# Weight splitting on GpSimd: whole units against pieces of two blocks

## The reference, cut to what matters

```python
h = rmsnorm(x, norm_mix)
proj = h @ w_in                       # q | k | v | g_ret | x_lru | y_lru | g_a | g_b
o, S_new = retention(rope(q), rope(k), v, S_ret)       # 4 heads, decay-weighted
ret_branch = (silu(g_ret) * groupnorm(o)) @ w_ret_out
xc = causal_conv(x_lru, conv_w, conv_b)
hl = rg_lru(xc, wa, wx, lambda)       # gated linear recurrence, block-diagonal gates
lru_branch = (gelu(y_lru) * hl) @ w_lru_out
x = x + (sigmoid(g_a) * ret_branch + sigmoid(g_b) * lru_branch) @ w_o
gu = rmsnorm(x, norm_ffn) @ w_gate_up
x = x + (silu(gu[:, :D_FF]) * gu[:, D_FF:]) @ w_down
```

## Time and profile before

| what | us |
|---|---|
| median of three runs | 2663.13 |
| lowest and highest | 2660.95, 2665.93 |
| the profiled execution, whole | 2665.94 |
| its span, first to last instruction | 2663.7 |
| PE busy | 2478.1 (93%) |
| DVE busy | 1368.6 (51%) |
| POOL busy | 1401.2 (53%) |
| ACT busy | 597.9 (22%) |

### The profile page before, as it was taken

How to read it: one execution, slowest core, us unless ns; L and a number is a source line. 1 busy time by engine, 2 the same in 40 slices (tenths; PEclk the granted TensorE clock), 3 DMA queues, 4 the chain that set the end, 5 groups by cost and what they waited for, 6 DMA issues and landing times.

```text
span 2663.7 us, 51524 instructions
## 1 busy us (share of the span) xinstructions
PE 2478.1 (93%) x19572; PEld 2406.2 (90%) x19572; DVE 1368.6 (51%) x1693; ACT 597.9 (22%) x849; POOL 1401.2 (53%) x845
## 2 busy tenths in 40 slices
PE   7799999978989999999997999999879999999997
PEld 7699989978889999999996999898779898999997
DVE  6455555587565543123254565655785656330333
ACT  2313131224251111001113132221434311110111
POOL 4254535444556656666652545454445565556664
PEclk9899999988999999999998999999999999999999
DMA  4535455312222222222245445362112222223222
GB/s 161 174 127 198 145 178 169 111 60 69 77 78 90 92 79 87 87 95 90 92 135 202 150 156 182 131 196 80 60 61 84 86 91 87 79 85 97 88 87 86
DMA packets 113009, 298.42 MB, mean 112 GB/s; under 512 B 11681, under 2 KB 12449, under 8 KB 112865
## 3 DMA queue, kind: packets, MB, share of 16 engines
q1 hardware_dynamic: 60480, 199.78, 23.1%
q10 hardware_dynamic: 52384, 96.56, 10.5%
HBM read 255.92 MB, written 40.38 MB: 111 GB/s over the span
## 4 chain that ended last, share of the span: by engine, by line
PE 76%; DVE 12%; DVEq 6%; issue 2%; ACTq 1%; ACT 1%; DMA 0%; POOL 0%; POOLq 0%
PE proj L310 69%; PE aux L463 2%; DVEq L1067 2%; DVE scratch L882 2%; PE aux L471 2%; PE aux L486 1%; PE aux L433 1%; DVE scratch L969 1%; DVE split_scratch L675 1%; DVE scratch L973 1%; DVEq L881 1%; ACTq L1386 1%; DVEq L972 1%; DVE scratch L668 1%; PE aux L450 1%
## 5 line engine op out<-in xcount | busy, mean ns | idle before, releaser
L296 POOL TENSOR_SCALAR w_high<-w_raw 128x1024 fp32r<-128x1024 f32 (+3 forms) x420 | 434.4, 1034 | 1176.9 <-PE proj L310 1167.0
L298 POOL TENSOR_TENSOR w_low<-w_raw,w_high 128x1024 fp32r<-128x1024 f32 (+3 forms) x420 | 966.4, 2301 | 62.2 <-issue 1.1
L310 PE MATMUL proj<-x_high,w_high 128*128 128x260 f32 x4096 | 849.1, 289 | 83.5 <-DVE scratch L951 35.2
L310 PE MATMUL proj<-x_high,w_low 128*128 128x260 f32 x4096 | 837.2, 286 | 0.0
L310 PE MATMUL proj<-x_low,w_high 128*128 128x260 f32 x4096 | 836.1, 286 | 0.0
L310 PEld LDWEIGHTS proj<-x_high,w_high 128*128 128x128 f32 x4096 | 645.2, 193 | 101.7 <-issue 49.1
L310 PE MATMUL proj<-split_scratch,w_high 128*128 128x260 f32 x4000 | 654.7, 286 | 38.2 <-DVE scratch L855 17.6
L310 PEld LDWEIGHTS proj<-x_high,w_low 128*128 128x128 f32 x4096 | 643.4, 192 | 0.0
L310 PEld LDWEIGHTS proj<-x_low,w_high 128*128 128x128 f32 x4096 | 643.4, 192 | 0.0
L310 PEld LDWEIGHTS proj<-split_scratch,w_high 128*128 128x128 f32 x4000 | 556.0, 191 | 43.7 <-DVE scratch L855 18.9
L310 PE MATMUL proj<-split_scratch,w_low 128*128 128x260 f32 x2000 | 406.4, 285 | 0.0
(11 more groups left out here) (145 smaller groups left out, 1941.9 us busy)
## 6 DMA issues: line engine op xcount, KB each, us to landing
w_raw<-in_wstream SPq DMA_DIRECT2D x252, 512.0 KB, 3.3
scratch<-in_sret ACTq DMA_DIRECT2D x64, 512.0 KB, 5.8
out_ret_s<-scratch ACTq DMA_DIRECT2D x64, 512.0 KB, 4.3
w_raw<-in_wstream SPq DMA_DIRECT2D x72, 448.0 KB, 3.2
w_raw<-in_wstream SPq DMA_DIRECT2D x48, 384.0 KB, 3.0
scratch<-v_rows ACTq DMA_DIRECT2D x64, 256.0 KB, 3.7
w_raw<-in_wstream SPq DMA_DIRECT2D x48, 320.0 KB, 2.7
out_ret_p<-scratch ACTq DMA_DIRECT2D x8, 512.0 KB, 2.8
```

Of the source, the lines that this page charges most:

```text
L296: pool.tensor_scalar(WH[:, j, w], WR[:, j, w], 1.0, 0.0, ALU.mult, ALU.add)
L298: pool.tensor_tensor(WL[:, j, w], WR[:, j, w], WH[:, j, w].bitcast(F32), ALU.subtract).then_inc(s["w_split"], 1)
L310: m = pe.matmul(out, wt[:, w, blk * P:(blk + 1) * P], x[xi], start=first and n == 0, stop=last and n == 2)
```

## The change

GpSimd no longer splits a unit in two instructions. A loop goes over the unit in pieces of two blocks (256 columns); each piece has its own rounding (TENSOR_SCALAR), drain and subtraction (TENSOR_TENSOR). A unit of odd size ends with a piece of one block. Only the last subtraction raises `w_split`; the waits ahead of the unit, the buffers and every other engine stay as they are.

```diff
+PIECE = 2
@@ in block.gpsimd
                         for k, n in enumerate(blocks):
-                            j, w = (base + k) % 2, slice(0, n * P)
+                            j = (base + k) % 2
                             u = layer * UNITS + base + k + i * len(blocks)
                             pool.wait_ge(s["w_used"], u + 2)
                             pool.wait_ge(w_ld[j], ...)
                             pool.sem_inc(s["go_pool"], 1)
-                            pool.tensor_scalar(WH[:, j, w], WR[:, j, w], 1.0, 0.0, ALU.mult, ALU.add)
-                            pool.drain()
-                            pool.tensor_tensor(WL[:, j, w], WR[:, j, w], WH[:, j, w].bitcast(F32),
-                                               ALU.subtract).then_inc(s["w_split"], 1)
+                            for b in range(0, n, PIECE):
+                                p = slice(b * P, min(b + PIECE, n) * P)
+                                pool.tensor_scalar(WH[:, j, p], WR[:, j, p], 1.0, 0.0, ALU.mult, ALU.add)
+                                pool.drain()
+                                m = pool.tensor_tensor(WL[:, j, p], WR[:, j, p], WH[:, j, p].bitcast(F32),
+                                                       ALU.subtract)
+                            m.then_inc(s["w_split"], 1)
```

## The result

The changed kernel takes 2836.08 us (median of four, 2835.01 to 2838.45) against 2663.83 us before: ratio 1.065, 95% interval 1.063 to 1.067. So it is 172 us slower; 99 were forecast, with 2675 to 2850 as the range.

A forecast was written before the change was run, and what follows sets the result against it. PE sets the time, and POOL's idle time cannot be saved up because each split has a deadline. Stage losses of 134 us less 35 returned by DVE gave 99, so 2762 us; range 2675 to 2850.

The forecast's parts named there:

- w_down: Feed-forward w_down stage: 32 units of 6 with no spare lose 0.98 us each, 31 us; units of 5 nothing.
- merge: Merge stage: 48 units of 7 lose 0.74 us each after 1.03 spare, 36 us.
- the cost of a further piece: Each further POOL piece adds drain and fixed parts of rounding and subtraction, less overlap: 0.49 us, ends 0.22 and 0.60.
- lru_out: lru_out stage: 14 units of 5 with 0.35 us spare lose 0.63 each, 9 us.
- gate and up: Gate and up stage: 44 pairs lose 0.57 us each, contending DVE instructions included, 25 us.
- heads: Heads stage: about 60 directly following units lose 0.02 us plus 0.4 for DVE each, 25 us.
- the return of 35: Shorter DVE waits give back 1.3 us for each of 16 y-tiles, plus 14 for convolution and w_o: 35 us.
- upper rival: Whole kernel much slower, 2870 us: 0.60 us a piece, 212 us lost, DVE gains nothing; chance 0.10.
- The rest: mostly hidden, 8: Remaining stages, bound by DVE: growth mostly hidden by POOL idle times of over 2.1 us; 8 us put down.
- The turn-round in gate and up: Unavoidable POOL idle time between splits, 0.66 us read from w_down; leaves gate and up 1.45 us spare a unit.
- faster: Whole kernel at 2631 us: further pieces cost near 0.22 us, DVE's shorter waits return 47; chance 0.09.
- The estimate of 0.41 a piece and 78 us: POOL's three reads a piece cost 0.26 us, with the drain 0.41; stage sums about 78 us instead of 134.

The follow-up runs named there:

- the early signal: Changed kernel, but TensorE may begin a unit when its first piece is split and waits for the whole ahead of the third block: 2629.23 us, ratio 0.9869.
- fixed-only kernel: Kernel before, units split whole, with two or three pairs of tiny GpSimd instructions and drains behind each split, before its signal: 2878.18 us, ratio 1.0795.

## Why the prediction was right in kind and low in size

The mechanism held. POOL's idle time could not be saved up: the early signal, which leaves POOL's work as it is and moves only the deadline, takes the loss away on balance (w_down keeps 4.6 and the merge 5.7 us). The durations were right (0.41 and 0.74 expected; 0.41 and 0.74 measured), and so was the cost of a further piece (0.49 against 0.51). PE waits for POOL 227 times for 176.8 us (some 250 times and over 100 us forecast). L1096 takes 0.70 and L1046 0.75 (below 1.3 forecast), L969 0.22 on average (below 1). PE's idle time in 530 to 680 us went from 30.3 to 24.6, so by far less than half.

Term by term, what was forecast and measured: merge 36 and 34.9; lru_out 9 and 9.8; gate and up 25 and 30.7; w_down 31 and 42.9; heads 25 and 51.1; all else 8 less the return of 35, so -27, and 1.0 measured. So the size was low by 73 us, and that it still fell into the range owes something to the range's width: 2836 is nearer to the upper rival's 2875 than to the forecast 2762. But that rival isn't what happened. It asked for 0.60 a piece and no return, and both were otherwise; of its terms for gate and up (54), merge (51), heads (45) and w_down (38), only heads and w_down came near. Two terms hold most of the error, heads (26) and the rest (23), and w_down (12) most of what is left:

- The heads. I gave every contending DVE instruction 0.4 us of POOL's time, from an instruction of 520 columns. The state update has 1024 columns and two SBUF inputs, and holds POOL up by 0.8 to 1.0; halving it gave back 21 of the 26 us by which the heads were too low.
- "The rest: mostly hidden, 8". In the fixed-only kernel, x-branch, y-branches and w_o lose 7.3 + 7.8 - 0.6 + 10.7 + 6.0 = 31 us. DVE is busy most there (123 of 150 us before), and POOL is held up most: in the changed kernel its instructions are 1.1 to 1.3 us a unit above their medians in the y-branches and the second x-branch, against 0.4 in gate and up. The return I had nearly right: in these stages the changed kernel is 30 us below the fixed-only one, against 35 forecast. So what I took for a gain of 27 was a gain of 30 on a loss of 31. L969 runs 20 times in the kernel and not 16; its mean fell from 1.55 to 0.22, so by the 1.3 that I took.
- The turn-round in gate and up. I read 0.66 from w_down and used it everywhere. In gate and up the rows after show 0.74 and 0.86 as the least idle time, since a loop's end lies in it every second unit: 0.28 a pair. With 0.12 for the piece's 0.51 that makes 0.97 for a pair in place of 0.57; measured are 6.64 + 5.92 - 11.53 = 1.03, so 45 us over 44 pairs. The stage's total, 30.7, came near the forecast 25 only because its first two units in each layer, 11.93 and 7.35 us before, take 6.53 and 6.03 now. The forecast had no term for this, and it is not a return of DVE's shorter waits: in the fixed-only kernel, where that DVE instruction at the end of w_o still takes 2.90, the two units take 6.62 and 6.03. There PE comes through w_o 6.0 us later, and DVE waits 0.8 to 1.0 us for PE ahead of most tiles, where before PE was never late for it there. So I read it as DVE's arrears at the end of w_o, which go when PE is slower. No run tests this by itself.
- w_down. A unit of 6 lost 0.88 in the first half of the feed-forward part, less than my 0.98, and 0.98 in the second. In the second half the unit of 5 lost 0.45 as well, which I had put within its spare time. DVE normalises alongside there, and POOL's instructions are 0.38 us a unit above their medians, against 0.05 in the first half. The step from the first half to the next stage cost 1.5 in each layer.

Of the rivals, "faster" asked for pieces below 0.3 us; the measured 0.51 ruled it out for this order of work. But its other half, DVE freed sooner, is real: pieces of four, which pay the fixed cost once, gain 34 us in the stages that gain and are 11 us faster in all. The estimate of 0.41 a piece and 78 us, worked out from the rule of the Trainium skill on read commands (GPSIMD Engine Reference, "Performance pitfalls for Q7 kernels"), gave too little; the measurements decide for 0.51. The rule of mutual exclusion in the Trainium skill (SBUF — State Buffer, "Who interferes with whom") is borne out from both sides: DVE's L1096 took 1.86 us beside POOL's long subtraction and takes 0.70 now, and POOL's subtractions take 1.20 and 1.13 beside DVE now, and 0.74 without it.

What stays open: how the return divides among DVE's single instructions, and what the fixed cost would take by itself. The fixed-only kernel has DVE's long waits and POOL's delays at once, so its 212 us are a cost beside them and not a pure one, and the 42 us are a difference of two kernels and no measurement of the return alone.

## What to carry to other kernels

An engine that is half idle between two buffers can't give away that half: read its idle time in front of each hand-over, subtract the least that ever occurs there, and compare what remains, stage by stage, with what you add. Add also what it loses to the engine that it takes turns with, by the length of that engine's instructions. Short instructions free the engine that waits for them, but each costs a fixed time; so cut only as fine as the spare time allows, and cut finer only where the waiting engine holds up the one that sets the time. Before paying for pieces at the deadline, hand over the first piece early: here that alone turned the same work from 172 us slower to 34 us faster.

## What the runs showed of the hardware

- On GpSimd a rounding and a subtraction on one column take 0.19 us each, and with the drain between them a pair costs 0.49 us from start to start; without a drain a following instruction starts only 0.03 to 0.04 us before the recorded end of the one ahead.
- Even an instruction of one column waits for VectorE: the tiny roundings take 305 ns on average against 190 undisturbed.
- A VectorE instruction with two SBUF inputs holds GpSimd up the longer, the more columns it has: 0.4 to 0.5 us with 520 columns (a subtraction of 0.74 took 1.20 and 1.13), 0.8 to 1.0 us with 1024 (1.52 for 0.74, 1.38 for 0.41).
- An additional wait of TensorE in every unit (420 in the run) cost nothing that shows: with it TensorE stayed busy 47.00 of 47 us in w_down, and a pair of units in gate and up took 11.53 us, as before.
